# Local attention steps of a fused transformer kernel: the order of VectorE's and ScalarE's work, and where six gate products stand

## The reference, cut to what matters

```python
s = jnp.where(mask, jnp.einsum('bnqhgd,bnkhd->bnhgqk', qb, kb), -jnp.inf)
m = jnp.maximum(jnp.max(s, axis=-1, keepdims=True), sink)
p = jnp.exp(s - m)
p = p / (jnp.sum(p, axis=-1, keepdims=True) + jnp.exp(sink - m))
o = jnp.einsum('bnhgqk,bnkhd->bnqhgd', p, vb)
...
h_m = mlstm_chunkwise(q_m, k_m, v_m, i_pre, f_pre)
y_m = jax.nn.sigmoid(o_m) * head_layer_norm(h_m, mlstm_norm_w)
merged = sigmoid(g_a) * (y_a @ w_branch_attn) + sigmoid(g_m) * (y_m @ w_branch_mlstm)
```

## Time and profile before

| what | value |
|---|---|
| median of 3 runs | 2705.8 us (2704.71 to 2706.97) |
| the profiled execution, its own time | 2707.68 us |
| its span on the core | 2705.9 us |
| mean granted TensorE clock | 0.993 |
| PE busy | 2619.3 us, 97% of the span |
| DVE, ACT, POOL busy | 1855.9, 1057.4, 1828.6 us |
| the stretch 1740 to 1860 us | PE busy 108.3 of 120.0 us |

### The profile page before, as it was taken

The page is one execution under the profiler, slowest core; times in us unless marked ns, Lnnn a source line. Parts: engine busy times, 40 slices in busy tenths (PEclk is TensorE's granted clock), DMA queues, the critical chain, the costliest instruction groups (busy, mean ns, idle before and its releaser), DMA issues.

```text
span 2705.9 us, 39410 instructions
## 1 busy us (share of the span) xinstructions
PE 2619.3 (97%) x12638; PEld 2089.2 (77%) x12638; DVE 1855.9 (69%) x2556; ACT 1057.4 (39%) x2146; POOL 1828.6 (68%) x1403
## 2 busy tenths in 40 slices
PE   8999999899999999999999999999999999999998
PEld 5777777677778888887777788877887888888887
DVE  6666687628888888887786465574458577666667
ACT  5544455435534333332443233564234322222212
POOL 4555432357698888886779984322468898888874
PEclk9999999999999999999999999999999999999999
DMA  4322232034221111115433435313443121111134
GB/s 150 106 86 86 86 94 71 16 117 152 79 59 55 55 54 54 54 59 170 136 127 112 121 107 186 98 55 123 165 132 133 43 63 53 57 54 54 55 128 141
DMA packets 98697, 253.55 MB, mean 94 GB/s; under 512 B 9423, under 2 KB 13296, under 8 KB 98292
## 3 DMA queue, kind: packets, MB, share of 16 engines
q1 hardware_dynamic: 72464, 186.41, 22.2%
q10 hardware_dynamic: 26084, 65.21, 6.7%
HBM read 211.20 MB, written 37.77 MB: 92 GB/s over the span
## 4 chain that ended last, share of the span: by engine, by line
PE 77%; POOL 8%; DVE 7%; ACT 4%; issue 3%; DMA 1%; POOLq 0%; ACTq 0%; DVEq 0%; SPq 0%
PE ps L1279 9%; PE ps L1281 9%; PE ps L1280 9%; PE ps L1650 7%; PE ps L1652 7%; PE ps L1651 7%; PE ps L1697 4%; PE ps L1699 4%; PE ps L1698 4%; PE ps L1370 3%; PE ps L1386 2%; POOL wl L1167 2%; PE ps L1401 1%; PE ps L1881 1%; POOL wl L1172 1%
## 5 line engine op out<-in xcount | busy, mean ns | idle before, releaser
L940 POOL CAST wh<-raw 128x1024 fp32r<-128x1024 f32 x139 | 149.6, 1076 | 471.7 <-PE ps L1281 414.9
L1279 PE MATMUL ps<-hh,wh 128*128 128x512 f32 x1040 | 438.0, 421 | 19.1 <-DVE hl L3316 10.9
L1281 PE MATMUL ps<-hh,wl 128*128 128x512 f32 x1040 | 410.5, 395 | 0.0
L1280 PE MATMUL ps<-hl,wh 128*128 128x512 f32 x1040 | 409.6, 394 | 0.0
L942 POOL TENSOR_TENSOR wl<-raw,wh 128x1024 fp32r<-128x1024 f32 x139 | 337.4, 2427 | 11.1
L1070 POOL TENSOR_TENSOR wl<-raw,wh 128x512 fp32r<-128x512 f32 x156 | 211.9, 1373 | 71.6 <-ACT wh L2511 70.6
L1279 PEld LDWEIGHTS ps<-hh,wh 128*128 128x128 f32 x1040 | 197.9, 190 | 73.4 <-issue 15.0
L1281 PEld LDWEIGHTS ps<-hh,wl 128*128 128x128 f32 x1040 | 197.2, 190 | 44.0
L1280 PEld LDWEIGHTS ps<-hl,wh 128*128 128x128 f32 x1040 | 198.2, 191 | 36.1 <-issue 3.4
L3703 DVE TENSOR_TENSOR hlf<-ps,hlf 128x512 f32<-128x512 f32 x252 | 171.4, 690 | 24.0 <-PE ps L1699 21.7
L971 POOL TENSOR_TENSOR arena<-arena 128x1023 f32<-128x1023 f32 (+7 forms) x64 | 114.7, 1803 | 105.0 <-ACT arena L2366 102.7
(11 more groups left out here) (479 smaller groups left out, 7229.6 us busy)
## 6 DMA issues: line engine op xcount, KB each, us to landing
raw<-weights SPq DMA_DIRECT2D x149, 512.0 KB, 3.6
raw<-weights SPq DMA_DIRECT2D x240, 256.0 KB, 2.6
arena<-w_ada SPq DMA_DIRECT2D x48, 512.0 KB, 3.8
arena<-gate_scratch ACTq DMA_DIRECT2D x25, 512.0 KB, 5.1
gate_scratch<-arena ACTq DMA_DIRECT2D x14, 512.0 KB, 2.6
gate_scratch<-sums_f ACTq DMA_DIRECT2D x17, 256.0 KB, 2.0
arena<-x_t ACTq DMA_DIRECT2D x1, 4096.0 KB, 14.1
x_scratch<-arena ACTq DMA_DIRECT2D x2, 2048.0 KB, 9.4
```

Source lines behind the costliest of these rows:

```text
L1279: pe.matmul(out, wh[:, slot, w], xh, start=start, stop=False)
L1280: pe.matmul(out, wh[:, slot, w], xl, start=False, stop=False)
L1281: return pe.matmul(out, wl[:, slot, w], xh, start=False, stop=stop)
```

## The change

On DVE, in every step, `w_norm`, `w_max` and `w_low` come first, and the work of the linear branch (`l_gate`, `l_rows`, `l_variances`, `l_means`) behind them. On ACT `l_unit(s)` of the local steps moves from the head of the step to its end. On PE six gate products (1, 2, 2, 1) stand behind the four values of step 8, where three stood behind the last; step 0 of the local attention then has two left in place of five. The number of instructions on every engine and the number of products stay the same.

```diff
-        ML_FILL, SW_FILL, SW_LEAD = (3, 2, 3, 2), (8, 11, 10, 6, 7, 5, 5, 4), 3
+        ML_FILL, SW_FILL, SW_LEAD = (3, 2, 3, 2), (8, 11, 10, 6, 7, 5, 5, 4), (1, 2, 2, 1)
@@ PE
-                    if s < ML_N:
-                        gate_fill(ML_FILL[t])
+                    if s <= ML_N:
+                        gate_fill((ML_FILL if s < ML_N else SW_LEAD)[t])
...
                     if n == 0:
-                        gate_fill(SW_LEAD)
-                        left -= SW_LEAD
+                        left -= sum(SW_LEAD)
@@ ACT
                 if n >= 0:
-                    l_unit(s)
                     turning = w_turned(n - 2) if 0 <= n - 2 < NB else []
...
                 if s >= 2 and s % 2 == 0 and s <= ML_N:
                     m_gate(s // 2 - 1)
-                if n < 0:
-                    l_unit(s)
+                l_unit(s)
@@ DVE
             for s in range(W_STEPS):
                 n = s - ML_N
+                if 0 <= n - 1 < NB:
+                    w_norm(2 * n - 2)
+                    w_norm(2 * n - 1)
+                if 0 <= n < NB:
+                    w_max(2 * n)
+                    w_max(2 * n + 1)
+                if 0 <= n - 3 < NB:
+                    w_low(n - 3)
                 for t in range(4):
...
                     if t == 2 and 0 <= s - 3 < ML_N:
                         l_means(s - 3)
-                if 0 <= n - 1 < NB:
-                    w_norm(2 * n - 2)
-                    w_norm(2 * n - 1)
-                if 0 <= n < NB:
-                    w_max(2 * n)
-                    w_max(2 * n + 1)
-                if 0 <= n - 3 < NB:
-                    w_low(n - 3)
```

## The result

The changed kernel takes 2723.44 us (median; 2721.57 to 2731.99), 1.0072 times the kernel before [1.0060, 1.0084]: on 2705.8 us that is 19.5 us more (the two medians lie 17.6 apart). Its profiled execution took 2721.57 us, with a span of 2719.7.

What follows compares the result with a forecast made beforehand. PE, busy for 97% of the span, was taken as the bound. Waits of -0.2 + 3.9 + 1.7 + 1.95 + 2.6 gave +10.0 us, with the clock +12.2: 2718.0 us, range 2709 to 2725.

Steps and rivals of the forecast that it cites:

- bank 4: Steps 2 to 5: the first turn waits for `l_gate`, now behind maxima that need the same step's scores; PE idles 3.9 in step 2.
- step 0: First local step: PE runs out of products and waits for `l_rows` before `l_transposes`; scores of step 1 start 0.8 us later.
- the clock: PE's clock drops behind long idle gaps; charged for steps 2 and 3, raising the sum from 10.0 to 12.2 us.
- Rival 4: More clock: borderline idles of steps 0, 4 and 5 also lower it, +4 more, 2722 us; chance 0.13.
- Lead products: Ahead of step 0: one product covers the small hole, two fit in the 1.77 us; scores start 0.1 us later.
- Done at 1754.6: Step 0, DVE: `l_rows` (0.2 and 1.12 us) ends at 1754.6, behind the maxima and `l_gate`.
- Step 1: Second local step: earlier maxima close PE's 1.00 us hole; steps 0 and 1 together give -0.2 us.
- Steps 2 to 5: First turns wait for `l_gate`; the steps lose +3.9, +1.7, +1.95 and +2.6 us before the clock.
- S+3.04: S is the start of a step's scores; DVE's first maximum was to start 3.04 us behind it.
- ACT's move: `l_unit` at the step's end costs nothing; without cover from DVE's maxima, up to 2.5 us in a step.
- Rival 3: Behind the stretch, PE's 4.16 us wait for POOL absorbs part of the loss: +8.0, 2713.8 us; chance 0.12.
- Rival 2: Bank 4 is free in time, so first turns do not wait for DVE's gating: -2.7 us, 2703.1; chance 0.08.

Runs made afterwards that it cites:

- lead_only: The kernel before with only the change's lead products (1, 2, 2, 1 among the last values): 2704.12 us, 1.0000.
- one_behind: The changed kernel with the last gate product of step 0 issued behind `l_transposes` instead of ahead: 2725.06 us, 1.0079.
- gate_first: The changed kernel with `l_gate` alone taken back to the front of DVE's local steps: 2709.56 us, 1.0015.
- awake: The changed kernel with nine unread matmuls of 512 columns on PE in each of the five holes: 2717.85 us, 1.0053.
- no_lead_again: The changed kernel with the three lead products in one group behind the last values as before, run once more for a profile: 2722.74 us, 1.0066.
- act_only: The kernel before with only ACT's move, `l_unit` at the end of the local steps: 2720.67 us, 1.0062.
- split_fill: split_order with three gate products also moved from step 1 to step 0: 2702.69 us, 0.9992.
- rows_between: split_fill with `l_rows` between the two maxima in steps 1 to 4: 2701.32 us, 0.9989.
- split_order: The changed kernel with DVE's local step as first norm, `l_gate`, second norm, maxima, `w_low`, rest; linear branch first in step 0: 2703.82 us, 1.0000.

## Why the direction was right, and why the size was not

The direction, the place and the mechanism of bank 4 were right. The size was not: 12.2 us forecast, 18.8 measured in the stretch and 19.5 by the ratio. 2705.8 times the ratio is 2725.3, just above the range; the median of 2723.44 is just inside. Two terms of the sum were mis-sized: step 0, where POOL's hold on DVE was left out (+0.8 forecast, +3.2 measured), and the clock, charged for two holes only (2.2 forecast, some 5.3 measured). Rival 4, more clock, came nearest.

- **Lead products.** Right in mechanism: the holes at the values shrink to 0.4 us, and lead_only shows the products missing behind the scores.
- **Step 0, a step that failed.** "Done at 1754.6" took 0.2 us for the small operation ahead of the rows. With POOL's subtraction in the way it was 1.84, and another, beside the cast, 0.89: 2.4 us. I had seen DVE's long operations in the trace of before and carried them into the range as a "hiccup" instead of asking what ran on POOL at the time. one_behind moves the cast away and the rows come on the forecast's time.
- **Step 1.** Forecast -1.0, measured -0.3. The 1.00 us hole did close, though DVE's order was not its only cause. PE was busy throughout and took 11.95 us for what takes 11.23 at full clock: 0.7 us came back as half clock behind the hole of step 0. one_behind confirms the size, with 11.16 at PEclk 0.98.
- **Steps 2 to 5.** Forecast +12.4 with the clock, measured +15.9. The mechanism is shown by gate_first. The waits alone were sized well: in awake, at clock 1.00, the four steps are 4.7, 1.8, 2.1 and 2.7 us longer than before, against 3.9, 1.7, 1.95 and 2.6. The 0.8 in step 2 is POOL again: its cast and its subtraction (from 1764.12) lie on a norm and a small product of DVE (1.83 and 2.32 us), and the first maximum starts at S+3.77 and not S+3.04.
- **The clock, the other step that failed.** 2.2 us charged for two holes. Measured were 4.6 in steps 2 to 5 (awake) and 0.7 in step 1. The holes of 2.69 and 2.68 us that I had left to the range cost 1.4 and 0.7. That they cost anything was chance: one such hole of one_behind and one of no_lead_again cost nothing.
- **ACT's move** added no wait in the whole change, as forecast: none of DVE or PE there is for `l_unit`'s results. act_only shows how much hung on the cover.
- **Rival 3**, part given back, falls: 890.2 us behind the stretch against 890.5. Rival 2 falls with the four waits of L2054.

Put together: 12.2 + 2.4 (step 0) + 0.8 (step 2) + 3.1 (clock) = 18.5 of 18.8 us; 0.3 stays unassigned. These are sums over one profiled execution of each kernel, and the clock alone moved single steps by 0.7 to 1.4 us between them. Moving DVE without ACT was not tried.

## What to carry to other kernels

When an operation that frees a PSUM bank is moved behind work that waits for matmuls of the same step, the bank's next matmul inherits that wait; look for it before counting what the move wins. How much of it counts depends on the step: at full clock step 2, which PE fills alone, lost 4.7 us, and step 3, where the hole was 3.56 us, lost 1.8. Two moves in two queues can each be free only because of the other, so cost each of them alone as well. An operation in a trace that is many times longer than its like is a term of the sum and no noise: look at what ended together with it on the other engines. It moves with the timing, so a change that takes it off one step can put it on the next, as in no_lead_again, gate_first and split_fill.

## What the runs showed of the hardware

**DVE held by GpSimd.** Operations of DVE on SBUF tiles grew while GpSimd's cast or subtraction of 128x1024 ran. Products of 128x4 grew from 0.16 to 0.89, 1.84, 2.32 and 2.36 us and ended 0.02 behind GpSimd's; groups of four TENSOR_SCALARs grew from 1.12 to 3.10, 3.24, 3.93 and 4.01 and ended 0.08 to 0.86 behind it. `l_gate`, with one operand in PSUM, and the reductions from PSUM did not grow. GpSimd can pay as well: its subtraction took 3.22 us instead of 2.34 where DVE's norm of 1.83 had started first.

The Trainium skill (SBUF — State Buffer, "Who interferes with whom") says that the two engines share a port pair as an exclusive lock, that a DVE instruction with two inputs in SBUF contends with a GpSimd instruction that reads SBUF, and that a reduction never does on trn2. The trace agrees: 0.16 against 1.84 for the products, and the reduction at 1758.19 in rows_between took its 1.22 us with the cast on top of it (1758.50 to 1759.54).

**The clock behind short holes.** The length of a hole alone did not decide whether PEclk fell to 0.50. Behind 2.69 us it fell in step 4 of the changed kernel and stayed at 1.00 in step 4 of one_behind and in step 5 of no_lead_again; behind 2.05 us it fell in split_order, behind 2.08 in lead_only and 2.19 in the kernel before it did not. Every hole of 3.2 us and more listed here was followed by half clock. It also fell with no hole: in the kernel before at about 145 us, where PE was busy for 13.92 of 14.00 us, behind 16 matmuls of one column (1.84 us) and a few small ones, and in the kernel after the same matmuls at the same place were followed by 1.00. With PE the bound, a fall cost 0.7 to 1.6 us in the steps above (2.6 in step 2 of one_behind, against awake).
